# Block results of the experts combined on chip: eight fp32 products after each turn of three blocks, in place of a table in DRAM

## The chip, the cores and the metric

The kernel runs on one core of one Trainium2 chip, with all data in fp32. The time is the device time of one launch, in microseconds. Before the change it is 2055.2 us, the median of 3 runs (2052.13 to 2055.3).

## What is computed

Two transformer-like blocks over 512 tokens of width 1024. The change lies in the last stage of the second one, a mixture of experts, with the sum into the residual and a last rms norm behind it. Every token is sent to two of 32 experts; an expert has a gate, an up and a down matrix of 1024x512, 1024x512 and 512x1024 fp32 numbers (2 MB each, written as 2048 KB in the profile).

```
gate = p_grp * softmax(top_val)                    # two weights for each token
expert_id = grp * 8 + top_idx                      # its two experts
def expert_block(xb, e):
    return (silu(xb @ w_gate[e]) * (xb @ w_up[e])) @ w_down[e]
ys = expert_block(rows of slot_tok, e) * slot_gate
out = zeros((T, D)).at[slot_tok].add(ys)
x = x + out ; y = rms_norm(x, final_norm)
```

## The kernel before, in words

**Routing.** Each expert's tokens are cut into blocks of 32 rows (`BS`). For each of the 1024 (token, choice) pairs, held as `C2` = 8 columns of 128 partitions, VectorE works out `rmod`, its row in a block, and `place`, the number of the block. The blocks are dealt out to three sets of weight buffers (`SETS` = 3): block c uses set c % 3, and blocks of one expert follow each other in the same set, so that a weight matrix is loaded only where the expert changes (`need`). In this run there are 54 blocks, 18 turns ("laps") of three.

**A block on TensorE** is four groups, always in this order: `gate_up(c)` (L1760: 16 fp32 products, 32 records), `next_rows(c+1)` (L1678: the next block's gathered rows are transposed), `down(c-1)` (L1778: 8 products, 16 records, into the bank `results[(c-1) % 3]`) and `turn_products(c)` (L1786: the gate and up results are folded and transposed, 8 records). Each fp32 product shows as two weight loads and two matmul records. In `gate_up` and `down` four products run beside each other in column tiles of 32.

**Beside it**: ScalarE copies the gate/up bank (L1792), copies the odd half of the down result to `y_odd` (L1802) and takes the silu (L1797). VectorE keeps the transposed rows (L1719), copies the next gather's indices (L1683), adds the two halves of the down result into `y_e`, 64 partitions x 512 (L1819), and multiplies silu by up (L1830), on which `down` waits. GpSimd issues the gather of the rows of a later block (L1860, L1671). The first three blocks' weights are loaded ahead. In the loop SyncE issues gate and up of block c+3 once `gate_up(c)` is done, and down of block c+2 once `down(c-1)` is done (L923); an issue whose `need` is 0 moves nothing. All these loads stand in one queue.

**Results.** ScalarE's queue stores each block's `y_e` to the DRAM table `y_rows`, 2 DMAs of 64 KB (L1812). The table has been filled with zeros, 8 MB, while the first feed-forward layer ran (L416; VectorE waits for it at L554). After the last block GpSimd gathers each token's two rows from the table with 8 indirect DMAs (L1924), VectorE adds them to `x_tok` times their gates (L1936, 8 instructions of 128x1024), ScalarE squares and sums (L1944), and VectorE scales (L1939, L1948, L1951), token tile by token tile (4 of 128 tokens), with one store of 512 KB each (L1953).

Of the kernel before, what the change touches and what calls it, by code (L numbers as in the profile page):

```python
# [32 lines left out]
BS = 32  # L33
MAX_BLOCKS = N_EXP + 2 * T // BS - 1
BLOCK_SHIFT = 5
SETS = 3
NO_ROW = 8 * T
Y_ROWS = -(-MAX_BLOCKS * BS // 128) * 128
SLOT_COLS = MAX_BLOCKS + 4
RING = 4  # L40
# [88 lines left out]
def build(nc, x_d, cols_d, rows_d, wdense_d, wff_d, wif_d, wr_d, strips_d, experts_d, out_d):  # L129
# [14 lines left out]
    s_wexp = [[sem(f"expert_weights_{n}_{b}") for b in range(SETS)] for n in ("gate", "up", "down")]  # L144
    s_y = [sem(f"block_results_stored_{b}") for b in range(SETS)]
    s_fill = sem("block_results_cleared")
    s_pick = [sem(f"results_gathered_{t}") for t in range(NT)]
    s_out = sem("output_stored")
# [56 lines left out]
    PO.run(po.memset(minus_half, -0.5))  # L205
    zeros = big[:, 44 * T:44 * T + D]
    cleared = PO.run(po.memset(zeros, 0.0))
    PO.run(po.affine_select(out=ident[:, :], in_=ident[:, :], compare_op=ALU.not_equal, fill=1.0, base=0,
# [140 lines left out]
    h_d = nc.dram_tensor("h_rows", (T, D), F32).ap()  # L349
    y_d = nc.dram_tensor("y_rows", (Y_ROWS, D), F32).ap()  # L350
    hid = Parts(big_r[:, 0:KF * T], big_r[:, KF * T:2 * KF * T])
# [37 lines left out]
    def ffn(first_in, first_out, ready, gain):  # L389
# [23 lines left out]
        hidden = DV.now()  # L413
        if gain == "mix_norm":
            AC.wait(cleared)
            ac.dma_start(y_d.rearrange("(n p) c -> p n c", p=128),  # L416
                         zeros.unsqueeze(1).to_broadcast([128, Y_ROWS // 128, D])).then_inc(s_fill, 16)

# [66 lines left out]
    n = 0  # L485
# [67 lines left out]

    dv.wait_ge(s_fill, 16)  # L554
    section(3, at["qk"] + RING, wdense_d, KD * 128, lambda i: qk_group(i, RING * T), 4, 0, 4)
# [1054 lines left out]
    rank, rdiv, rmod = sm(C2), sm(C2), sm(C2)  # L1610
    place, late, posf, pos = sm(C2), sm(C2), sm(C2), sm(C2)
    picks_jn = picks.rearrange("p (j n) -> p j n", j=2)
# [250 lines left out]
    act_copy(0, 0)  # L1863
    act_silu(0, 0, 2)
    with ac.Fori(0, laps["ac"]) as i:
        for c in range(1, SETS + 1):
            act_copy(i, c)
            act_odd(i, c - 1)
            act_silu(i, c)
            act_store(i, c - 1)  # L1870
    for c in range(1, SETS):
        act_copy(laps["ac"], c)
        act_odd(laps["ac"], c - 1)
        act_silu(laps["ac"], c)
        act_store(laps["ac"], c - 1)
# [30 lines left out]
    gate_up(laps["pe"], 1)
    next_rows(2)
    down(laps["pe"], 0)
    turn_products(laps["pe"], 1)
# [6 lines left out]
    for b in range(SETS):  # L1916
        po.wait_ge(s_y[b], laps["po"] * 32 + 48)
    po.wait_ge(PO.sem, laps["po"] * SETS + gathers_begun)
    po.tensor_tensor(zo, zc, zc, ALU.add)
    picked = [[big[:, (2 * t + j) * D:(2 * t + j + 1) * D] for j in range(2)] for t in range(NT)]  # L1920
    for t in range(NT):
# [147 lines left out]
```

## Time and profile before

| what | before |
|---|---|
| median of 3 runs | 2055.2 us |
| profiled execution: its own time | 2054.98 us |
| profiled execution: span of the core | 2053.7 us |
| mean granted TensorE clock | 0.937 of full |
| PE busy, share of the span | 1824.7 us (89%) |
| DVE busy | 863.6 us (42%) |
| the chain that ended last, by engine | PE 70%, DMA 13%, DVE 11% |

The span runs from the first to the last instruction on the core; the own time of the execution holds 1.3 us around it. PE is the matmul side of TensorE and PEld its weight loads; SPq, ACTq, POOLq are DMA issues of SyncE, ScalarE and GpSimd. All times inside the trace count from the start of the span.

### The profile page before, as it was taken

How to read it: one execution, taken by the hardware profiler on the slowest of the kernel's cores; microseconds unless marked ns; L12 is line 12 of the kernel's file. 1: busy time of each engine (PE TensorE's matmuls, PEld its weight loads, DVE VectorE, ACT ScalarE, POOL GpSimd, SP SyncE). 2: the span in 40 equal slices, each digit the busy share in tenths (PEclk: the TensorE clock that was granted, in tenths of full speed). 3: DMA queues.
4: the chain of work that ended last, by engine and by line, in shares of the span. 5: the costliest groups of instructions: out<-in, count | busy, mean ns of one | idle time of the engine just before them, and what ended most of it. 6: DMA issues, size and time to landing. Idle time of an engine off the chain costs nothing.

```text
span 2053.7 us, 27415 instructions
## 1 busy us (share of the span) xinstructions
PE 1824.7 (89%) x9686; PEld 1287.1 (63%) x9686; DVE 863.6 (42%) x1256; ACT 432.7 (21%) x794; POOL 992.7 (48%) x536
## 2 busy tenths in 40 slices
PE   5999999989999899999999798996877978969783
PEld 4888888877776578888888666664642423323331
DVE  5444443410254567444444489877341111111113
ACT  3111100100244432111100143551321211111112
POOL 5888887767544278888888523321211111101101
PEclk9999999999999999999999999997868988988897
DMA  3333363423221123333333222210579999999983
GB/s 126 97 97 93 105 262 98 141 79 98 66 62 52 32 85 95 97 93 101 92 109 98 72 60 64 72 52 21 212 287 412 374 408 402 410 415 398 413 358 133
DMA packets 56977, 346.00 MB, mean 168 GB/s; under 512 B 8474, under 2 KB 8858, under 8 KB 44896
## 3 DMA queue, kind: packets, MB, share of 16 engines
q1 hardware_dynamic: 44640, 315.12, 42.1%
q10 hardware_dynamic: 7968, 19.46, 2.6%
q0 software_dynamic: 4320, 10.78, 1.5%
q8 instruction: 29, 0.48, 0.1%
q14 instruction: 20, 0.16, 0.0%
HBM read 475.06 MB, written 19.66 MB: 241 GB/s over the span
## 4 chain that ended last, share of the span: by engine, by line
PE 70%; DMA 13%; DVE 11%; ACT 3%; issue 1%; POOL 1%; SPq 0%; DVEq 0%; ACTq 0%; POOLq 0%
PE bank L460 31%; DMA big<-w_up_in 13%; PE bank L431 12%; PE bank L1760 7%; PE bank L692 4%; PE bank L1266 3%; DVE big L1043 3%; PE bank L1778 2%; PE bank L479 2%; PE bank L1376 2%; PE bank L1786 1%; PE bank L610 1%; DVE state L1028 1%; PE bank L670 1%; PE bank L1678 1%
## 5 line engine op out<-in xcount | busy, mean ns | idle before, releaser
L277 POOL TENSOR_TENSOR weights_hi_parts<-ring,ones 128x1024 fp32r<-128x1024 f32 (+1 forms) x176 | 356.6, 2026 | 304.7 <-PE bank L460 139.1
L279 POOL TENSOR_TENSOR ring_parts<-ring,weights_hi_parts 128x1024 fp32r<-128x1024 f32 (+1 forms) x176 | 473.9, 2693 | 13.8
L460 PE MATMUL bank<-attention_buffers_parts,weights_hi_parts 128*128 128x512 f32 x832 | 329.4, 396 | 27.9 <-POOL ring_parts L279 17.6
L460 PE MATMUL bank<-state_parts,weights_hi_parts 128*128 128x512 f32 x832 | 326.8, 393 | 0.0
L460 PE MATMUL bank<-attention_buffers_parts,ring_parts 128*128 128x512 f32 x832 | 326.7, 393 | 0.0
L1760 PE MATMUL bank<-big,work 128*32 128x512 f32 x1440 | 231.7, 685 | 54.5 <-DMA big<-w_up_in 54.4
L431 PE MATMUL bank<-big_parts,weights_hi_parts 128*128 128x512 f32 x704 | 217.1, 389 | 1.2 <-POOL ring_parts L279 1.2
L460 PEld LDWEIGHTS bank<-attention_buffers_parts,weights_hi_parts 128*128 128x128 f32 x832 | 158.1, 190 | 64.6 <-POOL ring_parts L279 17.6
L864 POOL TENSOR_TENSOR ring_parts<-ring,weights_hi_parts 128x1024 fp32r<-128x1024 f32 x32 | 81.0, 2534 | 234.1 <-ACT weights_hi_parts L861 234.1
L1860 POOL TENSOR_TENSOR small<-small 128x1 f32<-128x1 f32 x51 | 9.7, 190 | 381.3 <-DVE small L1683 381.3
L460 PEld LDWEIGHTS bank<-state_parts,weights_hi_parts 128*128 128x128 f32 x832 | 158.3, 190 | 33.4 <-issue 0.8
L460 PEld LDWEIGHTS bank<-attention_buffers_parts,ring_parts 128*128 128x128 f32 x832 | 158.0, 190 | 33.5
L1719 DVE TENSOR_TENSOR work<-bank,cols 128x256 f32<-128x256 f32 x54 | 22.9, 425 | 306.0 <-PE bank L1678 304.9
L431 PEld LDWEIGHTS bank<-big_parts,weights_hi_parts 128*128 128x128 f32 x704 | 132.0, 188 | 29.2 <-POOL ring_parts L279 2.0
L1760 PEld LDWEIGHTS bank<-big,work 128*32 128x32 f32 x1440 | 63.6, 123 | 135.3 <-issue 129.6
L431 PE MATMUL bank<-big_parts,ring_parts 128*128 128x512 f32 x352 | 136.9, 389 | 0.0
L406 DVE TENSOR_TENSOR work<-bank,token_scale 128x512 f32<-128x512 f32 x44 | 30.4, 692 | 199.9 <-PE bank L460 199.9
L1043 DVE SCALAR_TENSOR_TENSOR big<-big,cols 128x512 f32<-128x512 f32 x120 | 106.5, 929 | 6.4 <-ACT big L1037 5.3
L315 DVE TENSOR_TENSOR big_parts<-work,big_parts 128x512 f32 (+1 forms) x44 | 82.9, 1884 | 42.3 <-ACT big_parts L313 42.3
L1792 ACT ACTIVATE weights_hi<-bank 128x512 f32<-128x512 f32 x54 | 32.3, 598 | 312.1 <-PE bank L1760 312.1
L1760 PE MATMUL bank<-attention_buffers,work 128*32 128x512 f32 x288 | 75.0, 667 | 24.0 <-DMA big<-w_up_in 23.4
L313 ACT ACTIVATE big_parts<-work 128x512 f32 (+1 forms) x44 | 27.9, 633 | 287.3 <-DVE work L408 287.3
(377 smaller groups left out, 2827.1 us busy)
## 6 DMA issues: line engine op xcount, KB each, us to landing
big<-w_up_in SPq DMA_DIRECT2D x54, 2048.0 KB
ring<-wdense_in SPq DMA_DIRECT2D x176, 512.0 KB, 3.6
state<-w_down_in SPq DMA_DIRECT2D x37, 2048.0 KB
big<-w_gate_in SPq DMA_DIRECT2D x36, 2048.0 KB
attention_buffers<-w_gate_in SPq DMA_DIRECT2D x18, 2048.0 KB
ring<-w_down_in SPq DMA_DIRECT2D x18, 2048.0 KB
ring<-wff_in SPq DMA_DIRECT2D x32, 704.0 KB, 4.1
y_rows<-big ACTq DMA_DIRECT2D x1, 8192.0 KB, 28.0
```

The source lines that it names most:

```text
L277: po.tensor_tensor(hi, raw, ones[:, 0:1].to_broadcast([128, words]), ALU.mult).then_inc(PO.sem, 1)
L279: po.tensor_tensor(lo, raw, hi.bitcast(F32), ALU.subtract) \
L315: return DV.step(dv.tensor_tensor(lo, raw, hi.bitcast(F32), ALU.subtract))
L431: m = pe.matmul(bank, x, y_, start=t + k + n == 0, stop=t == 1 and k == h - 1 and n == 2)
L460: m = pe.matmul(out, x, y_, start=j + n == 0, stop=j == len(pairs) - 1 and n == len(ts) - 1)
L479: m = pe.matmul(banks[t][:, :], x, y_, start=k + n == 0, stop=k == KD - 1 and n == len(ts) - 1)
L692: m = pe.matmul(banks[7][:, :], x, y_, start=k + t == 0, stop=k == KD - 1 and t == 2, skip_group_check=True)
L864: lo_made[n] = PO.step(po.tensor_tensor(lo, raw, hi.bitcast(F32), ALU.subtract))
L1043: last = DV.step(dv.scalar_tensor_tensor(dst, src, w, dst, ALU.mult, ALU.add))
L1266: m = pe.matmul(banks[bank][:, :], x, y_, start=k + j == 0, stop=k == KD - 1 and j == 2, skip_group_check=True)
L1376: m = pe.matmul(bank[:, :], x, y_, start=k == 4 and n == 0, stop=k == 3 and n == 2, skip_group_check=True)
L1760: m = pe.matmul(first_products[b][p:p + BS, :], xet[:, (k + odd) * BS:(k + odd + 1) * BS], sets[b][m_][:, (k + odd) * D_EXP:(k + odd + 1) ...
```

## The change

`y_rows`, its fill, its stores and its gathers go. The results of a turn of three blocks stay in SBUF as `lap_y`, 96 rows x 1024. A table `tab` holds, for each of the 96 rows and each lap, the token and the gate of that row; it comes from one product of 8 x 2 records at the start. In each lap VectorE writes `lap_hot`, 96 x 512: the gate where the row belongs to the token, else 0 (`dve_hot`). TensorE then multiplies `lap_hot` by `lap_y`: 4 token tiles x 2 halves = 8 fp32 products of K = 96, M = 128, N = 512 (`combine`), alternately into the banks `results[1]` and `results[2]`, and VectorE adds each one to `x_tok` (`dve_add`). Product n waits for the add of product n-2. `combine` stands behind `turn_products` of the second block of the next turn. The last turn has its 8 products in 8 banks behind the last `down`, with no wait between them. The loop on ScalarE, VectorE and TensorE begins two blocks in, instead of one.

```diff
-            ac.dma_start(y_d.rearrange("(n p) c -> p n c", p=128),
-                         zeros.unsqueeze(1).to_broadcast([128, Y_ROWS // 128, D])).then_inc(s_fill, 16)
-    dv.wait_ge(s_fill, 16)
...
+    PO.run(po.iota(token_row[:, :].bitcast(I32), [[1, T]], base=0, channel_multiplier=0))
+    numbered_tokens = PO.run(po.tensor_copy(token_row[:, :], token_row[:, :].bitcast(I32)))
...
-    DV.run(dv.scalar_tensor_tensor(posf, place, float(BS), rmod, ALU.mult, ALU.add))
-    DV.run(dv.tensor_copy(pos.bitcast(I32), posf))
+    DV.run(dv.tensor_scalar(lap.bitcast(I32), place, 43691.0, None, ALU.mult))
+    DV.run(dv.tensor_scalar(lap.bitcast(I32), lap.bitcast(I32), 17, None, ALU.logical_shift_right))
+    DV.run(dv.tensor_copy(lap, lap.bitcast(I32)))
+    DV.run(dv.scalar_tensor_tensor(lap_row, lap, float(-SETS), place, ALU.mult, ALU.add))
+    DV.run(dv.scalar_tensor_tensor(lap_row, lap_row, float(BS), rmod, ALU.mult, ALU.add))
...
     def down(i, c, steps=1):
-        pe.wait_ge(DV.sem, at_step(DV, DV_MUL, i, c))
+        pe.wait_ge(DV.sem, at_step(DV, DV_MUL[c % SETS], i, c))
+        if b == 1:
+            pe.wait_ge(s_added, i * 8 + 1)
...
-    def store(i, c):
+    def add_odd(c):
         for half in range(2):
-            ac.dma_start(y_d[bass.ds(i * (SETS * BS) + c * BS, BS), half * 512:half * 512 + 512],
-                         y_e[c % SETS][half * BS:(half + 1) * BS, :]).then_inc(s_y[c % SETS], 16)
+            p = slice(half * BS, (half + 1) * BS)
+            d = dv.tensor_tensor(lap_y[c % SETS * BS:(c % SETS + 1) * BS, half * 512:half * 512 + 512],
+                                 results[c % SETS][p, :], y_odd[p, :], ALU.add)
+        return d
...
+    def dve_hot(i):
+        dv.tensor_copy(sel[0:LAP, :], tab[0:LAP, bass.ds(i * 2, 2)]).then_inc(s_sel, 1)
+        dv.wait_ge(s_sel, i + 4)
+        dv.tensor_scalar(lap_hot, token_row[0:LAP, :], sel[0:LAP, 0:1], sel[0:LAP, 1:2], ALU.is_equal, ALU.mult)
+    def lap_product(n, bank):
+        t, half = n // 2, n % 2
+        pe.matmul(bank[:, :], lap_hot[:, t * 128:(t + 1) * 128], lap_y[:, half * 512:half * 512 + 512],
+                  start=True, stop=True).then_inc(s_prod, 1)
+    def combine(i):
+        pe.wait_ge(DV.sem, at_step(DV, DV_Y[0], i, 3))
+        for n in range(8):
+            if n > 1:
+                pe.wait_ge(s_added, i * 8 + n)
+            lap_product(n, results[1 + n % 2])
+    def dve_add(i):
+        for n in range(8):
+            dv.wait_ge(s_prod, i * 8 + (n + 1))
+            d = x_half(n // 2, n % 2)
+            dv.tensor_tensor(d, d, results[1 + n % 2][:, :], ALU.add).then_inc(s_added, 1)
...
     dve_rows(0, 0)
+    dv.tensor_tensor(by_slot(lap_hits), ... [128, C2, LAPS] ..., ALU.is_equal)
+    dv.tensor_tensor(by_slot(row_hits), ... [128, C2, LAP] ..., ALU.is_equal)
+    for k, v in enumerate((tok_id, gates)):
+        d = dv.tensor_tensor(row_values[:, :, :, k], by_slot(lap_hits), over_last(v, C2, LAPS), ALU.mult)
     dve_mul(0, 0, 2)
...
     with dv.Fori(0, laps["dv"]) as i:
-        for c in range(1, SETS + 1):
+        for c in range(2, SETS + 2):
             dve_rows(i, c)
-            dve_result(i, c - 1)
-            dve_mul(i, c)
+            if c == 4:
+                dve_mul(i, c)
+                dve_add(i)
+                dve_result(i, c - 1)
+            else:
+                dve_result(i, c - 1)
+                dve_mul(i, c)
+            if c == 2:
+                dve_hot(i)
...
     with pe.Fori(0, laps["pe"]) as i:
-        for c in range(1, SETS + 1):
+        for c in range(2, SETS + 2):
             gate_up(i, c)
             next_rows(c + 1)
             down(i, c - 1)
             turn_products(i, c)
+            if c == 4:
+                combine(i)
...
     down(laps["pe"], 2)
-            po.indirect_dma_start(picked[t][j], None, y_d[:, :], ...).then_inc(s_pick[t], 16)
+    pe.wait_ge(DV.sem, at_step(DV, DV_MUL[2], laps["pe"], 2) + 1)
+    last_banks = [banks[b] for b in (1, 2, 3, 0, 4, 5, 6, 7)]
+    for n in range(8):
+        lap_product(n, last_banks[n])
...
-            dv.wait_ge(s_pick[t], 32)
-            for j in range(2):
-                s = DE.run(dv.scalar_tensor_tensor(xt, picked[t][j], gates[...], xt, ALU.mult, ALU.add))
+            for half in range(2):
+                dv.wait_ge(s_prod, laps["dv"] * 8 + (2 * t + half + 1))
+                s = DE.step(dv.tensor_tensor(x_half(t, half), x_half(t, half), last_banks[2 * t + half][:, :], ALU.add))
```

## Rows read from the trace of the kernel before

**Rows 1.** Windows: length; busy PE, PEld, DVE, ACT, POOL; clock, DMA share, GB/s.
```profile
1600.00:1650.00 50.00, 45.81 (x406) 19.24 (x398) 8.47 (x24) 9.04 (x19) 6.65 (x12) 0.97 0.97 383
1800.00:1850.00 50.00, 35.49 (x260) 13.31 (x256) 5.59 (x16) 5.88 (x12) 4.43 (x8) 0.78 1.01 413
```
**Rows 2.** DMA queues from 1560 to 2000 us: packets, MB, share of 16 engines' time.
```profile
q1 hardware_dynamic: 11420, 166.14, 92.2%
q10 hardware_dynamic: 4608, 6.30, 4.0%
```
**Rows 3.** Timeline of ScalarE, gate/up copies (the end of each `gate_up`): start, duration.
```profile
1526.95 0.60 ACT L1792 ACTIVATE weights_hi<-bank 128x512 f32<-128x512 f32 x1 [22.95 <-PE bank L1760]
1532.34 0.60 ACT L1792 ACTIVATE weights_hi<-bank 128x512 f32<-128x512 f32 x1 [3.26 <-PE bank L1760]
1539.41 0.60 ACT L1792 ACTIVATE weights_hi<-bank 128x512 f32<-128x512 f32 x1 [3.32 <-PE bank L1760]
1553.44 0.60 ACT L1792 ACTIVATE weights_hi<-bank 128x512 f32<-128x512 f32 x1 [10.29 <-PE bank L1760]
1561.77 0.60 ACT L1792 ACTIVATE weights_hi<-bank 128x512 f32<-128x512 f32 x1 [4.58 <-PE bank L1760]
1580.32 0.60 ACT L1792 ACTIVATE weights_hi<-bank 128x512 f32<-128x512 f32 x1 [13.03 <-PE bank L1760]
1587.39 0.60 ACT L1792 ACTIVATE weights_hi<-bank 128x512 f32<-128x512 f32 x1 [3.32 <-PE bank L1760]
...
2014.96 0.60 ACT L1792 ACTIVATE weights_hi<-bank 128x512 f32<-128x512 f32 x1 [3.32 <-PE bank L1760]
```
**Rows 4.** Chain of waits in order of time: start, us, what.
```profile
1809.25 6.36 PE bank L1760 x32
1890.73 3.57 PE bank L1760 x32
```
**Rows 5.** The same chain: one fp32 product of 128x512 with 128 columns of weights.
```profile
1354.57 0.86 PE bank L1078 x2
```
**Rows 6.** Groups by form: busy us, mean ns | idle before.
```profile
L1078 PE MATMUL bank<-work,big 128*128 128x512 f32 x8 | 4.1, 592 | 0.0
L821 DVE TENSOR_TENSOR state<-state,bank 128x512 f32 x8 | 5.5, 687 | 2.9 <-PE bank L460 2.8
```
**Rows 7.** Timeline of one block with no wait for weights: start, duration.
```profile
2007.76 0.68 PE L1678 MATMUL bank<-ident,weights_hi 32*128 32x32 f32 x8
2008.47 0.42 DVE L1719 TENSOR_TENSOR work<-bank,cols 128x256 f32<-128x256 f32 x1 [3.58 <-PE bank L1678]
```
**Rows 8.** Timeline, routing and the first block.
```profile
1515.82 3.68 PE L460 MATMUL bank<-weights_hi,ones 128*128 128x67 f32 x16
1520.16 0.23 DVE L1713 SCALAR_TENSOR_TENSOR small<-small,work 128x64 int32<-128x64 f32 x1
1521.50 0.42 DVE L1719 TENSOR_TENSOR work<-bank,cols 128x256 f32<-128x256 f32 x1 [1.11 <-issue]
```
**Rows 9.** Waits around the fill of `y_rows` (250 to 330 us): us in total, times, longest.
```profile
PE bank L431 <- POOL ring_parts L279: 0.6, 1, 0.6
```
**Rows 10.** Timeline of the tail.
```profile
2016.54 1.10 PE L1786 MATMUL bank<-small,weights_hi 128*128 128x64 f32 x8
2017.36 0.68 DVE L1819 TENSOR_TENSOR ring<-bank,work 64x512 f32<-64x512 f32 x1 [5.40 <-ACT work L1802]
2017.99 0.29 DVE L1830 TENSOR_TENSOR weights_hi<-weights_hi,bank 128x128 f32<-128x128 f32 x1
2018.41 1.92 PE L1778 MATMUL bank<-state,weights_hi 128*32 128x512 f32 x16 [0.76 <-DVE weights_hi L1830]
2035.47 2.60 DVE L1936 SCALAR_TENSOR_TENSOR big<-big,small 128x1024 f32<-128x1024 f32 x2 [1.23 <-DMA big<-y_rows,small]
2038.80 1.28 DVE L1951 SCALAR_TENSOR_TENSOR big<-big,small,weights_hi 128x1024 f32<-128x1024 f32 x1
...
2049.74 1.29 DVE L1951 SCALAR_TENSOR_TENSOR big<-big,small,weights_hi 128x1024 f32<-128x1024 f32 x1
```

More of the change, by code:

```diff
@@ L37 @@
 NO_ROW = 8 * T
-Y_ROWS = -(-MAX_BLOCKS * BS // 128) * 128
 SLOT_COLS = MAX_BLOCKS + 4
@@ L144, in build @@
     s_wexp = [[sem(f"expert_weights_{n}_{b}") for b in range(SETS)] for n in ("gate", "up", "down")]
-    s_y = [sem(f"block_results_stored_{b}") for b in range(SETS)]
-    s_fill = sem("block_results_cleared")
-    s_pick = [sem(f"results_gathered_{t}") for t in range(NT)]
+    s_tab, s_sel = sem("rows_of_laps_summed"), sem("rows_of_lap_taken")
+    s_prod, s_added = sem("results_multiplied"), sem("results_added")
     s_out = sem("output_stored")
@@ L205, in build @@
     PO.run(po.memset(minus_half, -0.5))
-    zeros = big[:, 44 * T:44 * T + D]
-    cleared = PO.run(po.memset(zeros, 0.0))
     PO.run(po.affine_select(out=ident[:, :], in_=ident[:, :], compare_op=ALU.not_equal, fill=1.0, base=0,
@@ L349, in build @@
     h_d = nc.dram_tensor("h_rows", (T, D), F32).ap()
-    y_d = nc.dram_tensor("y_rows", (Y_ROWS, D), F32).ap()
     hid = Parts(big_r[:, 0:KF * T], big_r[:, KF * T:2 * KF * T])
@@ L413, in ffn @@
         hidden = DV.now()
-        if gain == "mix_norm":
-            AC.wait(cleared)
-            ac.dma_start(y_d.rearrange("(n p) c -> p n c", p=128),
-                         zeros.unsqueeze(1).to_broadcast([128, Y_ROWS // 128, D])).then_inc(s_fill, 16)
         def down(i):
@@ L1610, in build @@
     rank, rdiv, rmod = sm(C2), sm(C2), sm(C2)
-    place, late, posf, pos = sm(C2), sm(C2), sm(C2), sm(C2)
+    place, late, posf = sm(C2), sm(C2), sm(C2)
+    lap, lap_row, tab, sel = sm(C2), sm(C2), sm(2 * (MAX_BLOCKS // SETS)), sm(2)
     picks_jn = picks.rearrange("p (j n) -> p j n", j=2)
@@ L1650, in build @@
     slot_tok = sm(SLOT_COLS)
+    LAPS = MAX_BLOCKS // SETS
     tokens = slot_tok[0:BS, :].bitcast(I32)
@@ L1662, in build @@
     xet = work[:, D:D + KD * BS]
-    y_e = [ring[0:2 * BS, b * 512:(b + 1) * 512] for b in range(SETS)]
+    LAP = SETS * BS
+    lap_y, lap_hot, token_row = ring[0:LAP, 0:D], ring[0:LAP, D:D + T], sumsq
     y_odd = work[0:2 * BS, 2560:3072]
@@ L1727, in build @@
     DV.n += 4
-    ac.wait_ge(s_fill, 16)
-    for b in range(SETS):
-        ac.sem_inc(s_y[b], 16)
+    dv.sem_inc(s_added, 1)
     per = {"pe": 4, "ac": 3, "dv": 4}
@@ L1737, in build @@
     AC_GU, AC_Y, AC_SILU = range(1, 4)
-    DV_X, DV_IDX, DV_Y, DV_MUL = range(1, 5)
+    DV_X, DV_IDX = range(1, 3)
+    DV_Y, DV_MUL = (3, 4, 3), (4, 3, 4)
     def at_step(q, k, i, c):
@@ L1797, in act_silu, with act_odd @@
         ac.activation(hg3, turned_h[:, :, 0, :], ACT.Silu).then_inc(AC.sem, steps)
-    def act_odd(i, c):
+    def act_odd(i, c, first=False):
         ac.wait_ge(PE.sem, at_step(PE, PE_D, i, c + 1))
+        if not first:
+            ac.wait_ge(DV.sem, at_step(DV, DV_Y[c % SETS], i, c))
         ac.activation(y_odd, results[c % SETS][2 * BS:4 * BS, :], ACT.Copy).then_inc(AC.sem, 1)
-    def act_store(i, c):
-        ac.wait_ge(DV.sem, at_step(DV, DV_Y, i, c + 1))
-        store(i, c)
-    def store(i, c):
+    def add_odd(c):
         for half in range(2):
-            ac.dma_start(y_d[bass.ds(i * (SETS * BS) + c * BS, BS), half * 512:half * 512 + 512],
-                         y_e[c % SETS][half * BS:(half + 1) * BS, :]).then_inc(s_y[c % SETS], 16)
+            p = slice(half * BS, (half + 1) * BS)
+            d = dv.tensor_tensor(lap_y[c % SETS * BS:(c % SETS + 1) * BS, half * 512:half * 512 + 512],
+                                 results[c % SETS][p, :], y_odd[p, :], ALU.add)
+        return d
     def dve_result(i, c, steps=1):
         dv.wait_ge(AC.sem, at_step(AC, AC_Y, i, c + 1))
-        dv.wait_ge(s_y[c % SETS], i * 32 + (32 * (c // SETS) + 16))
-        dv.tensor_tensor(y_e[c % SETS], results[c % SETS][0:2 * BS, :], y_odd, ALU.add).then_inc(DV.sem, steps)
+        add_odd(c).then_inc(DV.sem, steps)
+    def dve_hot(i):
[17 more added lines that the diff above has]
+            dv.tensor_tensor(d, d, results[1 + n % 2][:, :], ALU.add).then_inc(s_added, 1)
     def dve_rows(i, c):
@@ L1864, in build @@
     act_silu(0, 0, 2)
+    act_copy(0, 1)
+    act_odd(0, 0, first=True)
+    act_silu(0, 1)
     with ac.Fori(0, laps["ac"]) as i:
-        for c in range(1, SETS + 1):
+        for c in range(2, SETS + 2):
             act_copy(i, c)
@@ L1869, in build @@
             act_silu(i, c)
[L1870 to L1875, printed above, removed]
+    act_copy(laps["ac"], 2)
+    act_odd(laps["ac"], 1)
+    act_silu(laps["ac"], 2)
     ac.wait_ge(PE.sem, at_step(PE, PE_HT, laps["ac"], 2) + 1)
+    ac.wait_ge(DV.sem, at_step(DV, DV_Y[2], laps["ac"], 2))
     ac.activation(y_odd, results[2][2 * BS:4 * BS, :], ACT.Copy).then_inc(AC.sem, 1)
-    ac.wait_ge(DV.sem, at_step(DV, DV_MUL, laps["ac"], 2) + 1)
@@ L1879, in build @@
-    store(laps["ac"], 2)
+    lap_hits, row_hits = ring[:, 0:C2 * LAPS], ring[:, 512:512 + C2 * LAP]
+    row_values = ring[:, 168:168 + 2 * C2 * LAPS].rearrange("p (c n k) -> p c n k", c=C2, k=2)
+    assert C2 * LAPS <= 168 and 168 + 2 * C2 * LAPS <= 512 and 512 + C2 * LAP <= RING * SLOT - WE
     dve_rows(0, 0)
-    dve_mul(0, 0, 2)
+    DV.wait(numbered_tokens)
+    dv.tensor_tensor(by_slot(lap_hits), iota_f[:, 0:LAPS].unsqueeze(1).to_broadcast([128, C2, LAPS]),
+                     over_last(lap, C2, LAPS), ALU.is_equal).then_inc(s_sel, 1)
@@ new lines, in build @@
+    dv.tensor_tensor(by_slot(row_hits), iota_f[:, 0:LAP].unsqueeze(1).to_broadcast([128, C2, LAP]),
+                     over_last(lap_row, C2, LAP), ALU.is_equal)
+    dv.wait_ge(s_sel, 1)
+    for k, v in enumerate((tok_id, gates)):
+        d = dv.tensor_tensor(row_values[:, :, :, k], by_slot(lap_hits), over_last(v, C2, LAPS), ALU.mult)
+    d.then_inc(s_sel, 1)
+    dve_mul(0, 0, 2)
+    dve_rows(0, 1)
+    dve_mul(0, 1)
+    dv.wait_ge(s_tab, 1)
+    dv.tensor_scalar(tab[0:LAP, :].rearrange("p (n k) -> p n k", k=2)[:, :, 0],
+                     results[2][0:LAP, 0:2 * LAPS].rearrange("p (n k) -> p n k", k=2)[:, :, 0], float(NO_ROW), None, ALU.add)
@@ L1883, in build @@
+    dv.tensor_copy(tab[0:LAP, :].rearrange("p (n k) -> p n k", k=2)[:, :, 1],
+                   results[2][0:LAP, 0:2 * LAPS].rearrange("p (n k) -> p n k", k=2)[:, :, 1]).then_inc(s_sel, 1)
+    dve_result(0, 0)
+    dv.wait_ge(s_sel, 3)
     with dv.Fori(0, laps["dv"]) as i:
-        for c in range(1, SETS + 1):
+        for c in range(2, SETS + 2):
             dve_rows(i, c)
-            dve_result(i, c - 1)
-            dve_mul(i, c)
-    dve_rows(laps["dv"], 1)
-    dve_result(laps["dv"], 0)
@@ L1890, in build @@
-    dve_mul(laps["dv"], 1)
+            if c == 4:
[7 more added lines that the diff above has]
+                dve_hot(i)
     dve_result(laps["dv"], 1, 3)
     dve_mul(laps["dv"], 2)
+    dve_hot(laps["dv"])
     dv.wait_ge(AC.sem, at_step(AC, AC_SILU, laps["dv"], 2) + 1)
-    dv.wait_ge(s_y[2], laps["dv"] * 32 + 16)
-    dv.tensor_tensor(y_e[2], results[2][0:2 * BS, :], y_odd, ALU.add).then_inc(DV.sem, 1)
+    add_odd(2).then_inc(DV.sem, 1)
@@ L1899, in build @@
     turn_products(0, 0, 2)
+    gate_up(0, 1)
+    next_rows(2)
+    pe.wait_ge(s_sel, 2)
+    product(results[2][0:LAP, 0:2 * LAPS],
+            [(row_hits[:, c * LAP:(c + 1) * LAP], ring[:, 168 + c * 2 * LAPS:168 + (c + 1) * 2 * LAPS]) for c in range(C2)]) \
+        .then_inc(s_tab, 1)
+    down(0, 0)
+    turn_products(0, 1)
     with pe.Fori(0, laps["pe"]) as i:
-        for c in range(1, SETS + 1):
+        for c in range(2, SETS + 2):
             gate_up(i, c)
@@ L1905, in build @@
             turn_products(i, c)
[L1906 to L1909, printed above, removed]
+            if c == 4:
+                combine(i)
     gate_up(laps["pe"], 2, rows_next=False)
@@ L1913, in build @@
     down(laps["pe"], 2)
[L1916 to L1921, printed above, removed]
-        for j in range(2):
-            c = j * NT + t
-            po.indirect_dma_start(picked[t][j], None, y_d[:, :],
-                                  bass.IndirectOffsetOnAxis(ap=pos[:, c:c + 1].bitcast(U32), axis=0)).then_inc(s_pick[t], 16)
+    pe.wait_ge(DV.sem, at_step(DV, DV_MUL[2], laps["pe"], 2) + 1)
+    last_banks = [banks[b] for b in (1, 2, 3, 0, 4, 5, 6, 7)]
+    for n in range(8):
+        lap_product(n, last_banks[n])
     AE, DE = Queue("act_end", ac, sem("act_end_steps")), Queue("dve_end", dv, sem("dve_end_steps"))
@@ L1933, in build @@
             xt = x_tok[:, t * D:(t + 1) * D]
-            dv.wait_ge(s_pick[t], 32)
-            for j in range(2):
-                s = DE.run(dv.scalar_tensor_tensor(xt, picked[t][j], gates[:, j * NT + t:j * NT + t + 1], xt, ALU.mult, ALU.add))
+            for half in range(2):
+                dv.wait_ge(s_prod, laps["dv"] * 8 + (2 * t + half + 1))
+                s = DE.step(dv.tensor_tensor(x_half(t, half), x_half(t, half), last_banks[2 * t + half][:, :], ALU.add))
         if t:
```

## Prediction

> **What bounds the kernel now.** I read three views of the experts' stretch, because everything the change touches lies there or behind it. First the windows: from 1550 to 1950 us the DMA engines are busy at 0.97 to 1.01 of their time in every window of 50 us, while PE's share and granted clock go up and down (0.97 and 0.78 of full in the two shown) [rows 1]. Second, who uses the DMA engines between 1560 and 2000 us: 92.2% of their time goes to the expert weights (q1), 4.0% to the stores of `y_rows` (q10), the rest to gathers [rows 2]. Third, the distance between the ends of consecutive `gate_up` groups. Where no weights are waited for it is 7.07 us (1580.32 to 1587.39; 32 of the 53 distances are under 7.2). Where weights are late it is longer: 14.03 us for block 3, 8.33 for block 4, 18.55 for block 5 [rows 3]. From the first to the last `gate_up` the trace takes 2014.96 - 1526.95 = 488.0 us, and 52 distances of 7.07 with the first one of 5.39 (there is no `down` in it) would take 373.0 us. So TensorE loses 115.0 us there to late weights. A part of that is no waiting but the lower clock of the group behind a wait: `gate_up` takes 6.36 us after a long wait and 3.57 us in a run of blocks [rows 4]. The stretch is bound by DMA, and TensorE has 115 us to spare in it.
>
> **What the change adds to a turn of three blocks.** Eight fp32 products of N = 512 with 128 weight columns. The same form stands in the chain with 0.86 us for one (two records) [rows 5]. K is 96 and not 128; no row shows that this helps, and I give it nothing. The floor of `combine` is thus 8 x 0.86 = 6.9 us. Products alternate between two banks, and product n waits for the add of product n-2. One round of a bank is: the first record 0.43, the second until its data are there 0.592 (mean of that form) [rows 6], the handoff to VectorE 0.03 (transposes end at 2008.44, VectorE starts at 2008.47) [rows 7], the add 0.687 (a 128x512 add of SBUF and a bank) [rows 6], the handoff back 0.13 (L1830 ends at 2018.28, `down` starts at 2018.41) [rows 10]: 1.87 us, and with a little for the weight load, which can't be ahead of a wait, 1.9 us for two products. They start at 0, 0.86, 1.9, 2.76, 3.8, 4.66, 5.7 and 6.56, and the last ends at 7.4 us. The other end, each product and its add with no overlap at all, is 8 x 1.87 = 15.0 us. I take 7.4: the two banks and the wait distance of two make the overlap explicit, and it is near the floor.
>
> Is VectorE ready? At the second block of a turn it takes `dve_mul` first, done 0.64 us after `turn_products` (2017.64 to 2018.28) [rows 10], and the first product's data come later than that. Behind the eight adds stand the two result adds; the next rows come only behind the next `gate_up` of 3.57 us, so nobody waits. The result add is two instructions of 32x512 instead of one of 64x512: the length goes by columns (0.687 for 128 partitions, 0.68 for 64 [rows 6, 10]), so +0.68 us for each block on an engine that is mostly idle; `down` comes 3.57 + 0.6 us behind `turn_products` and hides it. The same cover hides `dve_hot` (two instructions, under 0.9 us together; nothing needs them for two blocks). Without the cover, it would be 0.7 to 1.6 us for each block.
>
> There are 18 turns; 17 are combined in the loop: 17 x 7.4 = 125.8 us of TensorE's time. SyncE's issues stand behind `gate_up` and `down`, so each load is issued up to 7.4 us later; that is free as long as loads wait in the queue.
>
> **What it adds at the start.** Five short VectorE instructions in place of two, about +0.6 us, end before 1521.0; the transposed rows are taken at 1521.50 [rows 8]: hidden. The table's product is 16 records like those of L460, 3.68 us at the lower clock [rows 8], in front of `down(0)`. Its inputs (four VectorE instructions, some 1.9 us behind `dve_rows(0)`) are ready while `gate_up(1)` runs. +3.7 us in TensorE's order (0 if the first wait for weights hides it, 5 if VectorE is late).
>
> **What it removes.** The stores: 4.0 of 98.8 parts of DMA time, so the loads of the stretch from 1530 to 2010 us take about 480 x 0.96 = 461 us. The fill of 8 MB runs beside the down products of the first layer, where TensorE waits 0.6 us for POOL and never for a load [rows 9]: nothing, at most 1 us.
>
> **The stretch, added up.** TensorE's own order is now 373.0 + 3.7 + 125.8 = 502.5 us, and DMA needs 461. So TensorE becomes the bound, and what remains of waiting is only what can't be evened out. Before the first `combine` blocks 3 and 4 wait 6.96 and 1.26 us [rows 3], less the 3.7 above: 4.5. Block 5 waited 11.48 us, of which 7.4 is now `combine` and a part goes with the stores. Later ones are absorbed, because TensorE falls behind the queue. `down` can still be late where two experts change in a row, and the clock is low behind what waits are left. I put 8 us for all of it (0 to 15). The stretch: 502.5 + 8 = 510.5 against 488.0, +22.5 us.
>
> **The tail.** Before: `turn_products` of the last block ends at 2017.64 and the span ends at 2053.7, 36.1 us. After, on the same clock: the result add of block 52 starts at 2017.36 and takes 1.37, then the multiply, so `down` starts at 2019.15 instead of 2018.41 [rows 10] and ends at 2021.1. ScalarE's copy 0.60 [rows 3], two result adds 1.37, and the first product starts at 2023.3. First pair 1.72 and its last add: 2026.0. For each further tile: two adds 1.38, then mean, root, reciprocal and scaling as before. From the end of L1936 (2038.07) to the end of L1951 (2040.08) that is 2.0 us [rows 10], so 3.4 us a tile against 0.86 x 2 of TensorE: VectorE is the bound, 2026.0 + 3 x 3.4 = 2036.3, plus 2.0 for the last tile's scaling and 2.67 (2051.03 to 2053.7) for its store: 2041.1. The tail takes 23.5 us, 12.6 less (10 to 15). What is late next there is VectorE, not a DMA.
>
> Net: +22.5 - 12.6 = +9.9 us. The profiled execution took 2054.98 us (span 2053.7 and 1.3 around it), 0.2 below the median; so 2064.9, and I predict 2065.
>
> **A rule of the skill weighed.** In the window from 1600 to 1650 us PE is busy 45.8 of 50 us with short pauses between groups, and the granted clock is 0.97, mostly the 2.4 GHz level [rows 1]. The two-bank rounds would keep PE busy 1.72 of 1.9 us, about the same share, so the sum takes the full clock. The Trainium skill ("TensorE: Matmul & The Clock Gate", section "A second HAM failure mode: psum-queue depth-cycling") speaks against that: a kernel that cycled through PSUM banks paused so often that the clock went back and forth between its levels. By the row a product costs 0.86; by that rule, rival 3 below.
>
> **Rivals.**
> 1. *Faster: the products fit into the waits and DMA stays the bound.* For it: 115.0 us of spare time against 125.8, and the stores give back up to 19 us. Against it: the floor of 6.9 from rows 5. It decides below 7.4 - 9.9/17 = 6.8 us for a turn. With 6.5 us a turn and 2 us of waits: 373.0 + 3.7 + 110.5 + 2 - 488.0 = +1.2, less 12.6: 2044 us. Chance 0.11.
> 2. *Slower still: the rounds don't overlap as I lay them out* (a weight load or an issue pause of 0.2 us behind each wait). 8 x 1.1 = 8.8 us a turn: 17 x 1.4 = +24, so 2089 us. For it: TensorE can't load ahead of a wait. Chance 0.15.
> 3. *The products run at the lower clock.* `gate_up` shows a factor of 6.36/3.57 = 1.78 [rows 4]; 8 x 0.86 x 1.78 = 12.2 us a turn, +82: 2147 us. Against it: the waits that lower the clock now mostly go. Chance 0.04.
> 4. *No change*: the floor of 6.9 a turn, 17 x 0.5 = 8.5 less: 2056 us. Chance 0.08.
>
> The forecast holds the remaining 0.62, with a range of its own of 2059 to 2075 (7.1 to 7.9 a turn). Within 0.2% (4 us, about what a measurement can tell from none): 0.11, from rival 4 and the forecast's low edge. Faster 0.11, slower 0.78. Range for 8 in 10: 2051 to 2084, from the floor with a good tail to most of rival 2.
>
> **What would show it.** In the trace after: `gate_up` ends 7.07 apart inside a turn and 14.5 apart across `combine`; `combine`'s 16 records in 7.4 us, adds of 0.69; DMA share under 1 in the later windows and TensorE's clock near full with nearly no waits for `w_up`; no q10 traffic; last product about 12.6 us less from the end. If most turns still show waits for weights, or the distance across `combine` is under 13.9 or over 15.5 us, the forecast is wrong.

## The result, and the profile after

The changed kernel takes 2069.9 us (median of 4 runs, 2069.6 to 2071.9), the kernel before 2054.7 us (median of 4 too, 2052.1 to 2055.3): ratio 1.0079, 95% interval 1.0061 to 1.0096. It is 15 us slower; 10 were forecast. The profiled execution has a span of 2068.6 us against 2053.7. In the fences below, lines that don't bear on the text are left out.

First the page's busy times and queues of the changed kernel. Between 1560 and 2000 us the store queue q10 is gone and q1 (the weights) has 91.0% of the DMA time, where it had 92.2% [rows 2]:

```profile
PE 1930.8 (93%) x9990; PEld 1319.6 (64%) x9990; DVE 1002.4 (48%) x1491; ACT 432.7 (21%) x794; POOL 986.4 (48%) x528
...
q1 hardware_dynamic: 11093, 161.57, 91.0%
q0 software_dynamic: 2160, 3.56, 2.6%
```

Next the windows, with the columns of [rows 1]. In most of the stretch PE is busy for all of a window at full clock, and DMA has gaps. The window from 1700 to 1750 us is an exception, as is the one from 1550 to 1600: a wait for weights lies in it, the clock is 0.97 and DMA has no gap. So TensorE is the bound, but with the loads close behind it; that it is TensorE is what e1 and e2 test.

```profile
1600.00:1650.00 50.00, 50.00 (x378) 18.79 (x377) 21.74 (x44) 7.35 (x15) 5.56 (x10) 1.00 0.81 314
1650.00:1700.00 50.00, 50.00 (x352) 19.10 (x352) 22.67 (x45) 7.35 (x15) 5.57 (x10) 1.00 0.87 348
1700.00:1750.00 50.00, 47.98 (x323) 18.98 (x320) 19.41 (x39) 7.34 (x15) 5.57 (x10) 0.97 1.00 405
1800.00:1850.00 50.00, 50.00 (x352) 18.91 (x351) 22.67 (x45) 7.23 (x15) 5.24 (x11) 1.00 0.96 386
```

The waits of the stretch from 1520 to 2045 us (us in total, times, longest). The first answers to the 77.8 us in 20 waits that the same line had before; the second is TensorE's weight load waiting for the add that frees a bank:

```profile
PE bank L1758 <- DMA big<-w_up_in: 6.8, 2, 4.2
...
PEld bank L1828 <- DVE big L1844: 66.8, 102, 0.8
```

ScalarE's gate/up copies, that is the ends of `gate_up` of blocks 2 to 7 and 53, as in [rows 3]. Within a turn they are 7.07 us apart where no weights are waited for, and across each of the 17 groups of products 14.55 to 14.57:

```profile
1541.19 0.60 ACT L1792 ACTIVATE weights_hi<-bank 128x512 f32<-128x512 f32 x1 [3.32 <-PE bank L1758]
1550.88 0.60 ACT L1792 ACTIVATE weights_hi<-bank 128x512 f32<-128x512 f32 x1 [5.95 <-PE bank L1758]
1563.92 0.60 ACT L1792 ACTIVATE weights_hi<-bank 128x512 f32<-128x512 f32 x1 [9.29 <-PE bank L1758]
1578.49 0.60 ACT L1792 ACTIVATE weights_hi<-bank 128x512 f32<-128x512 f32 x1 [10.81 <-PE bank L1758]
1585.56 0.60 ACT L1792 ACTIVATE weights_hi<-bank 128x512 f32<-128x512 f32 x1 [3.32 <-PE bank L1758]
1592.63 0.60 ACT L1792 ACTIVATE weights_hi<-bank 128x512 f32<-128x512 f32 x1 [3.32 <-PE bank L1758]
...
2041.44 0.60 ACT L1792 ACTIVATE weights_hi<-bank 128x512 f32<-128x512 f32 x1 [10.81 <-PE bank L1758]
```

The timeline of one group of products. Products 2 and 3 load their weights only 0.05 us after the adds of 0 and 1 end (2031.96 and 2032.82), and the weight side has stood idle for 0.75 and 0.56 us before that. The adds start 0.86 and 1.04 us apart by turns:

```profile
2030.15 7.65 PE L1828 MATMUL bank<-ring 96*128 96x512 f32 x16
2031.27 0.69 DVE L1844 TENSOR_TENSOR big<-big,bank 128x512 f32<-128x512 f32 x1 [0.32 <-PE bank L1828]
2032.01 0.30 PEld L1828 LDWEIGHTS bank<-ring 96*128 96x128 f32 x2 [0.75 <-DVE big L1844]
2032.13 0.69 DVE L1844 TENSOR_TENSOR big<-big,bank 128x512 f32<-128x512 f32 x1 [0.17 <-PE bank L1828]
2032.87 0.30 PEld L1828 LDWEIGHTS bank<-ring 96*128 96x128 f32 x2 [0.56 <-DVE big L1844]
2033.17 0.69 DVE L1844 TENSOR_TENSOR big<-big,bank 128x512 f32<-128x512 f32 x1 [0.36 <-PE bank L1828]
```

The tail, which answers to [rows 10]: `turn_products` of the last block, the multiply, `down`, the result adds, the last eight products, the first two adds, and two of the four tiles' scalings:

```profile
2043.03 1.10 PE L1786 MATMUL bank<-small,weights_hi 128*128 128x64 f32 x8
2045.28 0.29 DVE L1855 TENSOR_TENSOR weights_hi<-weights_hi,bank 128x128 f32<-128x128 f32 x1
2045.69 1.92 PE L1778 MATMUL bank<-state,weights_hi 128*32 128x512 f32 x16 [1.56 <-DVE weights_hi L1855]
2048.39 1.38 DVE L1810 TENSOR_TENSOR ring<-bank,work 32x512 f32<-32x512 f32 x2 [2.17 <-ACT work L1903]
2049.82 8.83 PE L1828 MATMUL bank<-ring 96*128 96x512 f32 x16 [2.20 <-DVE ring L1810]
2051.25 0.69 DVE L1983 TENSOR_TENSOR big<-big,bank 128x512 f32<-128x512 f32 x1 [1.48 <-PE bank L1828]
2052.95 0.69 DVE L1983 TENSOR_TENSOR big<-big,bank 128x512 f32<-128x512 f32 x1 [1.02 <-PE bank L1828]
...
2056.54 1.28 DVE L1998 SCALAR_TENSOR_TENSOR big<-big,small,weights_hi 128x1024 f32<-128x1024 f32 x1
2059.62 1.28 DVE L1998 SCALAR_TENSOR_TENSOR big<-big,small,weights_hi 128x1024 f32<-128x1024 f32 x1
```

Eight products at full clock would take some 7.1 us, and these take 8.83. Short windows show where the clock was low. It is still 1.00 in the pause before the products, falls to 0.50 (the 1.2 GHz level) some 0.7 us after they have begun, and is back at 1.00 from about 2054 us:

```profile
2047.70:2049.80 2.10, 0.00 (x0) 0.00 (x0) 1.37 (x2) 2.01 (x3) 0.00 (x0) 1.00 0.02 4
2050.40:2050.60 0.20, 0.20 (x2) 0.14 (x1) 0.00 (x0) 0.00 (x0) 0.00 (x0) 0.88 0.00 0
2051.00:2052.00 1.00, 1.00 (x3) 0.48 (x2) 0.69 (x1) 0.00 (x0) 0.00 (x0) 0.50 0.00 0
2054.00:2055.00 1.00, 1.00 (x3) 0.38 (x2) 0.60 (x1) 0.82 (x2) 0.00 (x0) 1.00 0.00 0
```

All runs are compared by two lengths of the profiled execution: the stretch from the first to the last end of `gate_up`, and the tail from there to the end of the span. Each is one execution. How much a stretch moves by itself can be read from kernels with the same loop: e5, e6, e7 and e9 have 482.3 to 487.4, 5 us apart; the changed kernel and e8 have 514.2 and 513.7.

| kernel | stretch | tail | median time, us | ratio to before (95%) |
|---|---|---|---|---|
| before | 488.0 | 38.7 | 2052.7 to 2054.7 | 1 |
| changed | 514.2 | 27.2 | 2069.9 | 1.0079 (1.0061 to 1.0096) |
| e1 changed, no products in the loop | 475.3 | 27.2 | 2031.3 | 0.9889 (0.9872 to 0.9905) |
| e2 changed, stores back | 517.6 | 25.6 | 2072.2 | 1.0084 (1.0057 to 1.0111) |
| e3 before, no stores | 474.0 | 35.2 | 2040.0 | 0.9934 (0.9917 to 0.9951) |
| e4 four banks | 507.6 | 25.4 | 2063.2 | 1.0047 (1.003 to 1.0064) |
| e5 four banks, two bf16 parts | 487.4 | 29.3 | 2041.7 | 0.9939 (0.9926 to 0.9953) |
| e6 e5, multiply first | 484.9 | 26.4 | 2036.9 | 0.9921 (0.9904 to 0.9937) |
| e7 e5, pauses filled | 482.3 | 25.4 | 2037.9 | 0.9929 (0.9913 to 0.9946) |
| e8 changed, pauses filled | 513.7 | 25.5 | 2068.3 | 1.0072 (1.0055 to 1.0089) |
| e9 e6 and e7 | 484.8 | 24.7 | 2038.8 | 0.9929 (0.9915 to 0.9943) |

### The profile page after: what moved, and what is told of

Read it like the earlier page. It is cut to its first block, busy times and chain, and to the rows that moved or that the text cites. A ratio compares the mean times of both kernels' runs of the same rounds, so it can differ in the third digit from the quotient of the medians.

```text
span 2068.6 us, 28167 instructions
## 1 busy us (share of the span) xinstructions
PE 1930.8 (93%) x9990; PEld 1319.6 (64%) x9990; DVE 1002.4 (48%) x1491; ACT 432.7 (21%) x794; POOL 986.4 (48%) x528
## 4 chain that ended last, share of the span: by engine, by line
PE 81%; DVE 11%; DMA 3%; ACT 3%; issue 1%; POOL 1%; DVEq 0%; ACTq 0%; SPq 0%; POOLq 0%
PE bank L451 30%; PE bank L422 12%; PE bank L1758 9%; PE bank L1828 6%; PE bank L1778 4%; PE bank L682 4%; PE bank L1256 3%; DVE big L1033 3%; PE bank L1786 2%; PE bank L470 2%; PE bank L1366 2%; DMA state<-w_down_in 1%; PE bank L1671 1%; DMA big<-w_up_in 1%; PE bank L600 1%
## 5 line engine op out<-in xcount | busy, mean ns | idle before, releaser
L275 POOL TENSOR_TENSOR ring_parts<-ring,weights_hi_parts 128x1024 fp32r<-128x1024 f32 (+1 forms) x176 | 473.9, 2692 | 13.8
L1758 PE MATMUL bank<-big,work 128*32 128x512 f32 x1440 | 201.1, 608 | 5.7 <-DMA big<-w_up_in 4.2
L1828 PE MATMUL bank<-ring 96*128 96x512 f32 x288 | 138.9, 621 | 2.2 <-DVE ring L1810 2.2
L1810 DVE TENSOR_TENSOR ring<-bank,work 32x512 f32<-32x512 f32 x108 | 73.5, 681 | 79.6 <-ACT work L1804 76.7
L1844 DVE TENSOR_TENSOR big<-big,bank 128x512 f32<-128x512 f32 x136 | 93.4, 687 | 35.4 <-PE bank L1828 35.4
L1758 PEld LDWEIGHTS bank<-big,work 128*32 128x32 f32 x1440 | 51.2, 111 | 86.7 <-issue 84.0
## 6 DMA issues: line engine op xcount, KB each, us to landing
big<-strips_in ACTq DMA_DIRECT2D x1, 3072.0 KB, 12.6
```

Source lines behind the costliest of these rows:

```text
L275: po.tensor_tensor(lo, raw, hi.bitcast(F32), ALU.subtract) \
L1758: m = pe.matmul(first_products[b][p:p + BS, :], xet[:, (k + odd) * BS:(k + odd + 1) * BS], sets[b][m_][:, (k + odd) * D_EXP:(k + odd + 1) ...
L1828: pe.matmul(bank[:, :], lap_hot[:, t * 128:(t + 1) * 128], lap_y[:, half * 512:half * 512 + 512], start=True, stop=True).then_inc(s_prod, 1)
L1844: dv.tensor_tensor(d, d, results[1 + n % 2][:, :], ALU.add).then_inc(s_added, 1)
```

## The experiments

**e1, the loop's products and their adds left out** (only the last turn keeps its own).

```diff
-            if c == 4:
-                combine(i)
...
-                dve_add(i)
```

> The changed kernel without the eight products and eight adds of the 17 turns in the loop (left out; the last turn keeps its own). Theory: TensorE is the bound of the experts' stretch in the changed kernel, and takes 17 x 7.49 = 127 us for the products; without them the loads are the bound again, 4% faster than before because the stores are gone: stretch from the first to the last gate_up 470 to 478 us instead of 514.2, time 2026 to 2036 us, so the products cost 35 to 44 us of 127. Rival A (products simply add up, nothing is hidden): 2070 - 127 = 1943 us. Rival B (the stores took nothing from the loads): stretch 488, 2044 us.

Measured 2031.3 us, stretch 475.3. The products take 17 x 7.49 = 127.3 us of TensorE, and the stretch is only 38.9 us shorter without them. The medians say the same, 38.6 us. So some 88 us of the products lay in time that TensorE would have waited. Without them the DMA share is back at 0.96 to 1.01 and PE has gaps:

```profile
1600.00:1650.00 50.00, 46.08 (x424) 18.81 (x416) 14.26 (x36) 9.41 (x19) 7.76 (x14) 1.00 0.96 377
1850.00:1900.00 50.00, 48.26 (x425) 19.38 (x423) 16.04 (x39) 9.31 (x20) 6.66 (x12) 0.97 1.01 404
```

**e2, the stores put back into the changed kernel; e3, the stores left out of the kernel before.**

```diff
+            ac.dma_start(y_d[bass.ds(i * (SETS * BS) + c * BS, BS), half * 512:half * 512 + 512],
+                         lap_y[...]).then_inc(s_y[c % SETS], 16)
```

> The changed kernel with each block's result also stored to DRAM in two DMAs of 64 KB, as before (nothing reads it; the last block's store is left out). Theory (TensorE is the bound, DMA engines have slack of up to 19% in some windows): 2 to 8 us more, 2072 to 2078 us. Rival (the loads are still the bound and the change gained the stores' 17 us): 2087 us.

> The kernel before with the stores of the block results left out of the loop (the gathers at the end then read zeros). Theory (its stretch is bound by DMA, stores are 4% of the DMA time): stretch 472 to 478 us instead of 488, and some 2 us less before the gathers, time 2036 to 2044 us. Rival (stores run beside the loads at no cost): 2053 us.

The same stores cost 14.0 us of the stretch where the loads bind (e3: 474.0 against 488.0; the medians give 13.8 us with the tail). Where TensorE binds, they cost 3.4 us of the stretch (e2: 517.6 against 514.2). The medians give 2.3 us there, which can't be told from nothing: e2's four runs go from 2064.4 to 2075.7 us, and the intervals overlap. What e2 does show is that the 17 us of its rival (2087 us) are not there. So one resource had given way to the other. In e3 the tail is 3.5 us shorter too. The gathers begin 7.2 us behind the last `gate_up` instead of 10.0, since they need not wait for the last stores.

**e4, four banks for the products.**

```diff
+    turn_banks = (results[1], results[2], banks[1], banks[2])
...
-            if n > 1:
-                pe.wait_ge(s_added, i * 8 + n)
-            lap_product(n, results[1 + n % 2])
+            if n > 3:
+                pe.wait_ge(s_added, i * 8 + (n - 2))
+            lap_product(n, turn_banks[n % 4])
```

> The changed kernel with the eight products of a turn in four banks instead of two, so that product n waits for the add of product n-4. Theory (the two-bank round of 1.9 us is 0.18 over two products of 0.86, and TensorE is the bound): 6.9 instead of 7.49 us a turn, 17 x 0.6 = 10 us less, of which the loads may take back 2: 2060 to 2063 us. Rival (the pause is not the handoff, or the loads bind): 2068 to 2070 us.

`gate_up` ends are 13.99 us apart across the products: 6.92 us a turn against 7.49, 9.7 us over 17 turns. The stretch is 6.6 us shorter and the time 6.7 us less than the changed kernel's, at the upper edge of what was expected. The rest goes to the loads: waits for `w_up` are 6 now and 9.2 us, where the changed kernel has 2 and 6.8. The adds now start 0.86 us apart, as the products alone allow:

```profile
2023.36 7.08 PE L1828 MATMUL bank<-ring 96*128 96x512 f32 x16
2024.47 0.69 DVE L1846 TENSOR_TENSOR big<-big,bank 128x512 f32<-128x512 f32 x1 [0.32 <-PE bank L1828]
2025.33 0.69 DVE L1846 TENSOR_TENSOR big<-big,bank 128x512 f32<-128x512 f32 x1 [0.17 <-PE bank L1828]
```

**e5, e4 with each product of the loop as two bf16 products.** The results, times their gates, are held as a high and a low bf16 part (some 16 bits of the fp32 number's 24), and the table row is 0 or 1.

```diff
+        ac.activation(lap_hi, lap_y, ACT.Copy, scale=sel[0:LAP, 1:2]).then_inc(s_hi, 1)
...
+            d = dv.scalar_tensor_tensor(lap_lo[half], lap_y[:, h], sel[0:LAP, 1:2], lap_hi[:, h], ALU.mult, ALU.subtract)
...
+        pe.matmul(bank[:, :], w, lap_hi[:, half * 512:half * 512 + 512], start=True, stop=False)
+        pe.matmul(bank[:, :], w, lap_lo[half], start=False, stop=True).then_inc(s_prod, 1)
```

> The kernel with four banks, and in the loop's 17 turns the product made of two bf16 products: lap_hot is 0 or 1, the gate goes into the results, and these are split into a high and a low bf16 part (ScalarE one 96x1024 copy, VectorE two 96x512 instructions a turn, both beside gate_up). The last turn stays fp32. One bf16 pass of 512 columns is taken like an fp32r pass, 0.21 us, so a product costs 0.43 instead of 0.86 us; with the adds of 0.69 behind it in four banks a turn costs about 4.0 us instead of 7.49. Theory (TensorE falls below the loads, which are the bound as in the run without products at 2031 us): 2040 us (2036 to 2046), faster than both kernels. Rival (the clump of products still pushes each turn by its full length, as where TensorE is the bound): 2070 - 17 x 3.5 = 2010 is excluded by the loads; if the adds set the turn at 8 x 0.72 = 5.8 us: 2048 to 2052 us.

2041.7 us: faster than both kernels. Across the products `gate_up` ends are 10.92 us apart, 3.85 us a turn. A bf16 pass takes 0.22 us, and only the last three products wait for an add (0.22, 0.38 and 0.48 us of idle weight load; the fence has the second):

```profile
1706.23 0.38 PE L1855 MATMUL bank<-scale_halves,ring_halves 96*128 96x512 bf16 x1
1706.23 0.10 PEld L1856 LDWEIGHTS bank<-ring_halves 96*128 96x128 bf16 x1
1706.45 0.38 PE L1856 MATMUL bank<-ring_halves 96*128 96x512 bf16 x1
...
1706.95 4.86 DVE L1879 TENSOR_TENSOR big<-big,bank 128x512 f32<-128x512 f32 x8
...
1708.87 0.10 PEld L1855 LDWEIGHTS bank<-scale_halves,ring_halves 96*128 96x128 bf16 x1 [0.38 <-DVE big L1879]
```

The stretch is 12.1 us above that without products (487.4 against 475.3), for 17 x 3.85 = 65 us of work; e6, e7 and e9, with the same loop, are 7 to 10 us above it. e5 changes the number type and not the banks against e4, and the results of the experts now have fewer bits. Its tail of 29.3 us was the longest of the new ones, which asked for the experiments that follow.

**e6, e7, e8, e9: the tail.** In the last turn TensorE waits 1.56 us for the multiply and 2.20 us for the result adds. e6 puts the multiply ahead of the result add of the block before. e7 (on e5) and e8 (on the changed kernel) put products that nobody reads into both pauses. e9 is e6 with the filler of the second pause, two products. The fences show e6's main edit and that of e7 and e8.

```diff
-    dve_result(laps["dv"], 1, 3)
-    dve_mul(laps["dv"], 2)
+    dve_mul(laps["dv"], 2, 3)
+    dve_result(laps["dv"], 1)
```
```diff
+    pe.wait_ge(AC.sem, at_step(AC, AC_GU, laps["pe"], 2))
     turn_products(laps["pe"], 2)
+    fill(1)
     down(laps["pe"], 2)
+    fill(2)      # matmul(banks[1], ident, token_row), n times
```

> The kernel with two bf16 parts; in the last turn VectorE multiplies silu by up before the result add of the block before, not behind it. Theory (the last down waits 1.55 us for the multiply, of which the 1.38 us of the result add are half hidden): the last down starts 0.7 to 0.8 us earlier, tail 0.7 us shorter if the clock is as before. From the last gate_up to the end of the span 28.6 us instead of 29.3, time 2041. If the shorter pause also keeps the clock high (the last eight products took 10.2 us here, 7.1 us at full clock): 26 to 27 us. Rival (the multiply is not what down waits for): 29.3 us.

> The kernel with two bf16 parts, with three fp32 products that nobody reads put into TensorE's two pauses in the last turn (one of 0.86 us behind turn_products, two behind the last down), where TensorE waits 1.6 and 2.2 us. Theory (the low clock of the last products follows from TensorE's waiting just before): the last eight products take 7.2 instead of 10.2 us, and from the last gate_up to the end 26 to 27.5 us instead of 29.3: some 2.5 us less. Rival (the clock there has nothing to do with the pauses, or the filler only delays): 29.3 to 30 us.

> The same three filler products in the changed kernel itself, whose last eight products took 8.8 us (7.1 at full clock) and whose tail from the last gate_up is 27.2 us. Theory: 25.4 us, as in the run with four banks, where the clock stayed full; time 1.8 us less, 2068. Rival: 27.2 us or more.

> The kernel with two bf16 parts, the multiply first in the last turn, and two filler products behind the last down. Theory: both effects of the tail add up: the last down 0.75 us earlier and the last products at full clock, from the last gate_up to the end 24.7 us (29.3 with neither, 26.4 and 25.4 with one); time 2035 to 2038 us, the fastest of all. Rival (the earlier down only makes the pause before the products longer, 25.4 us or more).

The last eight products in e5, then in e7:

```profile
2023.73 10.16 PE L1861 MATMUL bank<-ring 96*128 96x512 f32 x16 [2.18 <-DVE ring L1817]
```
```profile
2019.15 7.13 PE L1861 MATMUL bank<-ring 96*128 96x512 f32 x16 [0.29 <-DVE ring L1817]
```

With the filler they take 7.13 us in all three kernels that have it. Without it they take 8.83 (changed, e1, e6) or 10.16 (e5), with the clock at 0.50 for a part of them, but also 7.13 in e2 and e4, which have nearly the same pauses (1.66 and 2.12 us in e2, 1.56 and 2.20 in e4). So the filler was not needed each time. That it is what keeps the clock up fits all nine kernels, but with two of six at full clock without it, three of three with it is no proof.

The tails: e7 has 25.4 us, less than the 26 to 27.5 expected; e8 has 25.5 and e9 24.7, as expected. e6 alone has 26.4, 2.9 less than e5. 0.7 of that is the earlier `down` (its pause is 0.83 us instead of 1.55), as expected, and most of the rest is clock, since `down` takes 1.92 us instead of 2.82 and the products 8.83 instead of 10.16. The shorter pause did not give the full clock, though. In the medians these 2 us drown: e6, e7 and e9 can't be told apart (0.9921, 0.9929, 0.9929), and e8 is 1.6 us below the changed kernel with intervals that overlap. e9 was expected at 2035 to 2038 us and as the fastest; at 2038.8 us it missed both.

## Why the prediction was right, point by point

- *The bound changes from the loads to TensorE.* Right: windows, waits, and e1 to e3 from three sides.
- *A group of products: 7.4 us a turn.* 7.49, 127.3 us instead of 125.8. The round of a bank is 1.90 us, as laid out, and e4 shows that it was this round: 6.92 without it, where 6.9 was the floor given.
- *The start and what remains of waiting: 3.7 + 8 us.* 13.9 us measured (514.2 - 373.0 - 127.3), split otherwise than forecast. Block 2 comes 8.55 us behind block 1 instead of 7.07: the table's product costs 1.5 us. I had priced it at 3.7 from a row of 67 columns at the lower clock [rows 8]; it has 42 columns and ran at full clock:

```profile
1533.11 1.55 PE L451 MATMUL bank<-ring 128*96 128x42 f32 x16
```

  The other 12.4 us are waits, and the lower clock behind them, at block 3 (9.69 - 7.07 = 2.6), block 4 (13.04 - 7.07 = 6.0), block 19 (3.2) and block 21 (0.7). Block 5 absorbed its wait inside its 14.57 us, as said. The three distances up to block 4 sum to 31.3 us. They were 29.4 before, without the table's product, and are 29.4 in e1 and e4, 30.3 in e2 and 31.0 in e5 with it. So this sum is set by when the load of block 4 lands, which the chain of waits shows as well, here for the changed kernel and then for e4:

```profile
1533.32 25.07 DMA big<-w_up_in
```
```profile
1532.54 23.23 DMA big<-w_up_in
```

  It follows that the wrong price of the table's product cost nothing, which is luck: the 2.2 us too many in it would have been spent on waiting in any case. What was forecast too low is the sum, by 1.9 us (31.3 against the 29.4 of before that the forecast kept). Over all eleven kernels it goes from 28.8 to 31.3; why the first loads vary was not tested.
- *The stretch.* Terms together: 22.5 forecast, 26.2 measured; 1.5 of the difference is the products, 2.2 the start and the waits.
- *The tail: 23.5 us from the end of `turn_products`, 12.6 less.* 24.5 us (2044.13 to 2068.6), 11.6 less. The order of steps and `down`'s start (1.56 us after `turn_products`, 1.5 forecast) were right. The first two adds came at 2051.25 and 2052.95 instead of 0.86 us apart, because the clock was at 0.50 from some 0.7 us after the first product's start, behind two pauses that the change itself puts there. e8 has the full clock there and is at 25.5 - 2.7 = 22.8 us by the same measure (2.7 us lie between the last `gate_up` and the end of `turn_products`). For the tiles behind it 3.1 us were needed and not 3.4 (2056.54 to 2059.62). So two errors worked against each other here: 0.9 us too many for three tiles, and 1.7 us (e8) of low clock that had no term.
- *Sum.* +26.2 - 11.6 = +14.6, and the first `gate_up` ends 0.3 us later: +14.9 against +9.9. Of the 5 us missed, 3.7 are the stretch and 1.0 the tail.
- *Rival 1* (the products fit into the waits) fell: a turn costs 7.49 us and not 6.5. At e5's 3.85 us the loads bind again. Its price and that of *rival 4* (2056 us at 6.9 us a turn) were too low, as e4 shows: 6.92 us a turn, and 2063.2 us. At that price of a turn the start and the waits take 17.0 us of the stretch (507.6 - 373.0 - 117.6) and not 11.7. Nor do the stores give back the 19 us that rival 1 counted, but 14 (e3). *Rival 2* (no overlap as laid out) fell by the 7.49. *Rival 3*, the low clock for the products, was wrong for the loop, where the clock is 1.00 in three of the windows shown, with the pauses of the rounds in them, and 0.97 in the one with a wait for weights. It was in part right for the last eight, which I had priced at full clock. The rule of the Trainium skill that stood beside this rival ("TensorE: Matmul & The Clock Gate", "A second HAM failure mode: psum-queue depth-cycling") did not hold for these rounds: the section tells of bf16 products, and these are fp32. In e5, whose products are bf16 and use four banks, the clock is 1.00 from 1600 to 1650 us too.

## What to carry to other kernels

Time in which an engine waits is a budget and not a gift: add up what the change puts on that engine and compare it with all its waiting in the stretch (126 against 115 us here), then ask where the waits lie, for work at fixed places can't use those before it. Taking traffic off a bound resource pays (14 us here) only while it is the bound; the same stores cost some 3 us, or nothing that the medians can tell, once TensorE was. When the bound has moved, the lever is the new engine's own work: halving the time of its products (0.86 to 0.43 us each), at the price of some bits, together with two more banks turned +15 us into -11 (e5).

## What the runs show of the hardware

- Not expected: the clock over the last products differed from kernel to kernel behind much the same pauses of 1.6 and 2.2 us. Eight products took 7.1 us in e2 and e4, 8.8 in the changed kernel and e1, 10.2 in e5; with filler products 7.1 in e7, e8 and e9.
- Not expected: the clock did not fall while TensorE paused but after it had begun again. In the changed kernel that was some 0.7 us into the last products; in e5 some 0.9 us into the last `down`, and it came back only near 2029.8 us, 10 us later.
- As priced: 96 rows in the product instead of 128 bought nothing, 0.86 us as in [rows 5].
- As priced: an fp32 result add of 32x512 takes as long as one of 64x512 (0.69 us each, two in 1.38).
